# Order of VectorE and ScalarE work at the start of the first delta head in a hybrid decoder trunk

## The reference

```
qkv = silu(causal_conv(qkv_in, conv_w))            # width 4, over time
q = l2norm(q) * B_DK**-0.5;  k = l2norm(k * valid) # 4 heads of 128
beta = sigmoid(beta_in) * valid
log_a = -exp(a_log) * softplus(decay_in + dt_bias)
o = chunk_gated_delta(q, k, v, log_a, beta)        # chunked, WY form
y_b = gated_head_norm(o, g_in, norm_w)             # rmsnorm(o) * silu(gate)
...
ys = stack([y_a, y_b, y_c])
gates = sigmoid(gate_logits)                       # (tokens, 3, D)
merged = sum(gates * (ys @ w_branch), axis=branch)
h = h + merged @ w_out
```

## Time and profile before

| | us |
|---|---|
| median of 3 runs | 1070.21 |
| lowest and highest | 1069.61, 1072.17 |
| the profiled execution, device time | 1069.23 |
| its span, first to last instruction | 1067.4 |
| TensorE busy | 1018.4 (95%) |
| VectorE busy | 552.6 (52%) |
| ScalarE busy | 310.1 (29%) |

### The profile page before, as it was taken

The page is one execution under the profiler, slowest core; times in us unless marked ns, Lnnn a source line. Parts: engine busy times, 40 slices in busy tenths (PEclk is TensorE's granted clock), DMA queues, the critical chain, the costliest instruction groups (busy, mean ns, idle before and its releaser), DMA issues. The chain is left out here.

```text
span 1067.4 us, 20881 instructions
## 1 busy us (share of the span) xinstructions
PE 1018.4 (95%) x8985; PEld 723.0 (68%) x8985; DVE 552.6 (52%) x1088; ACT 310.1 (29%) x579; POOL 112.5 (11%) x109
## 2 busy tenths in 40 slices
PE   9999999989999999999999999999998999787887
PEld 8888888767787877878776676544566665445544
DVE  6577786868569478387464364332344322111114
ACT  2345354624244343344332042010110111100013
POOL 3322222000000000000100100000001222211110
PEclk9999999999999999999999999999999999989899
DMA  9232223231332232142222221174847999999976
GB/s 265 69 85 63 61 61 80 60 64 41 81 64 63 60 84 62 41 88 58 60 60 60 60 61 60 40 275 154 364 163 275 414 415 414 415 416 415 418 312 247
DMA packets 111967, 174.76 MB, mean 164 GB/s; under 512 B 9011, under 2 KB 87100, under 8 KB 103554
## 3 DMA queue, kind: packets, MB, share of 16 engines
q1 hardware_dynamic: 99010, 134.93, 36.6%
q10 hardware_dynamic: 7136, 27.33, 6.5%
q0 software_dynamic: 5728, 11.14, 3.9%
HBM read 169.16 MB, written 12.60 MB: 170 GB/s over the span
## 5 line engine op out<-in xcount | busy, mean ns | idle before, releaser
L823 PE MATMUL ps<-arena 128*128 128x256 f32 x1008 | 237.6, 385 | 0.0
L823 PEld LDWEIGHTS ps<-arena 128*128 128x128 f32 x1008 | 185.2, 190 | 27.3 <-issue 2.8
L1517 DVE TENSOR_TENSOR arena<-arena 128x256 f32<-128x256 f32 (+6 forms) x202 | 111.4, 593 | 49.4 <-ACT arena L1308 32.7
L853 PE MATMUL ps<-arena 128*128 128x264 f32 x400 | 124.3, 393 | 0.8 <-DVE gates L1649 0.8
L2413 PE MATMUL ps<-arena,gates 128*64 128x256 f32 (+1 forms) x1088 | 107.2, 356 | 17.0 <-DMA arena<-in_expert_w_up 16.5
L854 PE MATMUL ps<-arena 128*128 128x264 f32 x400 | 121.7, 386 | 0.0
L2413 PEld LDWEIGHTS ps<-arena,gates 128*64 128x64 f32 x1088 | 74.6, 145 | 55.7 <-DMA arena<-in_expert_w_up 24.9
L847 PE MATMUL ps<-yT,arena 128*128 128x512 f32 x192 | 84.8, 596 | 2.1 <-DVE gates L1649 1.4
L854 PEld LDWEIGHTS ps<-arena 128*128 128x128 f32 x400 | 76.1, 190 | 13.1
L853 PEld LDWEIGHTS ps<-arena 128*128 128x128 f32 x400 | 71.9, 191 | 13.1 <-issue 2.8
L2592 DVE COPY gates<-ps 128x1024 f32<-128x1024 f32 x15 | 18.4, 1224 | 100.9 <-PE ps L2394 100.9
(11 more groups left out here) (379 smaller groups left out, 1396.4 us busy)
## 6 DMA issues: line engine op xcount, KB each, us to landing
arena<-in_w_in SPq DMA_DIRECT2D x68, 512.0 KB, 3.9
arena<-in_expert_w_gate SPq DMA_DIRECT2D x27, 1024.0 KB
arena<-in_expert_w_up SPq DMA_DIRECT2D x27, 1024.0 KB
arena<-in_expert_w_down ACTq DMA_DIRECT2D x16, 1024.0 KB, 34.2
arena<-in_w_branch SPq DMA_DIRECT2D x12, 512.0 KB, 4.2
arena<-in_expert_w_down SPq DMA_DIRECT2D x6, 1024.0 KB, 11.2
C<-in_expert_w_gate SPq DMA_DIRECT2D x5, 1024.0 KB
gates<-in_expert_w_up SPq DMA_DIRECT2D x5, 1024.0 KB
```

The costliest lines, as they stand in the source:

```text
L823: mm = t.matmul(dst, wt[:, k, :], rhs[:, k, :], start=(k == 0), stop=(k == KH - 1))
L853: t.matmul(dst[:, 0:HALF], wt, uT[:, k, 0:HALF], start=(k == 0), stop=(k == KD - 1))
L1517: v.tensor_tensor(out_, a_, b2, op).then_inc(*q.did(name))
```

## The change

The first delta head (r = 0) gets another order; heads 1 to 3 keep theirs. On VectorE, the old head's end (y1, y) and the memset go ahead of the query convolution. That is cut in two: q0 and q1 before the keys' difference tk, q2 and q3 behind it. The gate product and the weight sums S1 and S2 go behind km and kr. On ScalarE the exponential of the merge gate goes from behind the softplus to behind the square kk. `convolve` takes a range of steps for this.

```
--- before.py
+++ after.py
@@ -524,8 +524,9 @@
                                      [f"Z{l}" for l in LB[1:]] + ["nw"])] + each(B_R - 1, ["oo", "ln", "ri"]))
         queries = ["q0", "q1", "q2", "q3"]
         b_dve = Order("b_dve", [x for r in range(B_R) for x in
-                                each(r - 1, ["oq"] if r else []) + each(r, ["k0", "k1", "k2", "k3"]) + (each(r - 1, ["y1", "y"]) if r else each(r, queries + ["pad"])) +
-                                each(r, ["tk", "km", "kr"] + (queries if r else []) + ["dif", "min", "kn", "kb", "Ei", "Es", "tq", "qm", "qr",
+                                each(r - 1, ["oq"] if r else []) + each(r, ["k0", "k1", "k2", "k3"]) + (each(r - 1, ["y1", "y"]) + each(r, ["tk", "km", "kr"] + queries) if r else
+                                                         each(r, ["pad"] + queries[0:2] + ["tk"] + queries[2:] + ["km", "kr"])) +
+                                each(r, ["dif", "min", "kn", "kb", "Ei", "Es", "tq", "qm", "qr",
                                          "U", "Ua", "Ub", "v0", "v1", "v2", "v3", "gc", "kbg", "kd", "tv", "Da", "vm", "vr", "QK", "Db",
                                          "tg", "vb", "qg", "E1", "D1", "g"] +
                                      [x for l in LB[1:] for x in ((f"E{l}", f"D{l}") if l < LEVELS - 1 else (f"E{l}",))] + chain)] +
@@ -1401,12 +1402,12 @@
                 if r == 0:
                     a.wait_ge(*a_dve.after(f"y1.{A_R - 1}"))
                 softplus(b_act, ("abk", "ek", "lk"), r, b_em[:, 0:TOK], b_kbg[:, 0:TOK])
-                if r == 0:
-                    gate_end("a", A_R - 1)
                 a.wait_ge(*b_dve.after(f"tk.{r}"))
                 a.activation(b_em[:, 0:TOK], b_em[:, 0:TOK], ACT.Exp).then_inc(*b_act.did(f"sk.{r}"))
                 a.wait_ge(*b_dve.after(f"kr.{r}"))
                 a.activation(b_kb, b_kf, ACT.Square).then_inc(*b_act.did(f"kk.{r}"))
+                if r == 0:
+                    gate_end("a", A_R - 1)
                 a.wait_ge(*b_pe.after(f"ssk.{r}"))
                 a.activation(b_em, pair(4), ACT.Ln, bias=eps_c).then_inc(*b_act.did(f"lnk.{r}"))
                 a.wait_ge(*b_act.after(f"lnk.{r}"))
@@ -1777,10 +1778,10 @@
                     v.tensor_tensor(q_bg, q_beta, q_eg, ALU.mult).then_inc(*dve0.did("bg"))
                     v.tensor_tensor(q_kd, q_gl, q_g, ALU.subtract).then_inc(*dve0.did("dk"))
 
-            def convolve(s, c, src, r):
+            def convolve(s, c, src, r, steps=range(4)):
                 n = "qkv".index(s)
                 v.wait_ge(*block_done("b", s, r))
-                for j in range(4):
+                for j in steps:
                     at = R_CONV + (3 - j) * 12 + n * 4 + r
                     wc = rowsT[:, at:at + 1]
                     if j == 0:
@@ -1815,16 +1816,23 @@
                 if r:
                     b_finish(r - 1)
                 else:
-                    convolve("q", cq, wide(1), r)
                     a_finish(A_R - 1)
-                    gate_part("a", A_R - 1)
                     v.wait_ge(*a_dve.after(f"y.{A_R - 1}"))
                     v.memset(padding(), 0.0).then_inc(*b_dve.did("pad.0"))
+                    convolve("q", cq, wide(1), r, range(0, 2))
+                if r:
+                    mix_weights("S1", "b", r)
+                less("k", b_em[:, 0:TOK], ck, b_em[:, 0:TOK], r)
+                if r:
+                    mix_weights("S2", "b", r)
+                else:
+                    convolve("q", cq, wide(1), r, range(2, 4))
                     v.wait_ge(*b_dve.after("pad.0"))
-                mix_weights("S1", "b", r)
-                less("k", b_em[:, 0:TOK], ck, b_em[:, 0:TOK], r)
-                mix_weights("S2", "b", r)
                 unit("k", b_kf, ck, b_em, r)
+                if r == 0:
+                    mix_weights("S1", "b", r)
+                    gate_part("a", A_R - 1)
+                    mix_weights("S2", "b", r)
                 if r:
                     convolve("q", cq, wide(1), r)
                 v.wait_ge(sem("decay_rows"), 16 * r + 16)
```

24 lines of the change are left out of this document (15 added, 9 removed).

## The result

| | before | changed |
|---|---|---|
| median, us | 1070.26 (5 runs) | 1064.83 (5 runs) |
| lowest to highest | 1069.61 to 1072.17 | 1062.91 to 1067.21 |
| the profiled execution | 1069.23 | 1067.21 |

The ratio is 0.9946, with an interval of 0.9926 to 0.9967: 5.4 us faster by the medians, where 4.2 were forecast. The same kernel in a second comparison gave 1064.95 against 1069.88, a ratio of 0.9954 (0.9940 to 0.9968). Two executions of the kernel before, in later series, took 1469.5 and 2613.1 us; they are left out of every median here.

The account below looks back on a forecast made before the run. TensorE's own stream was taken as the bound. ssk 3.01 us earlier plus 1.50 from the clock, less a 0.33 wait at the first level product, gave 4.18: median 1070.21 to 1066.0 us, range 1064.2 to 1068.8.

Parts of the forecast that it names:

- What bounds: Whole kernel: TensorE's own stream sets the time; its longest gap, 4.40 us before ssk.0, costs 5.90 with the clock.
- y1 first: VectorE, first delta head: y1 starts when the old head's root is ready, at 229.26 us; softplus then starts 3.49 earlier.
- The steps to ssk: VectorE and ScalarE, y1 through keys to ssk.0: starts 3.01 us earlier, gap 1.39; rival of longer steps, chance 0.12.
- the Trainium skill's rule on the flush: VectorE, split query steps: independent neighbours would save nothing, putting km about 0.1 to 0.2 us later.
- The clock: TensorE between ssk.0 and KK.0: no fall after a 1.39 us gap, giving back 1.50; rival, falls anyway, chance 0.09.
- lnk behind the exponential: ScalarE: lnk waits for the gate's exponential until 238.35 us, costing it 0.7, hidden because kb is ready before KK.
- To the end: Mixers and expert stage: the head's whole 4.18 us gain is kept; rival, no effect or taken back, chance 0.11.

Follow-up runs that it names:

- Fill only: Kernel before with eight instead of six steps of block v ahead of ssk on TensorE in the first delta head; 1067.62 against 1070.01 us, ratio 0.9980.
- the exponential late: Changed kernel with the gate's exponential on ScalarE moved from ahead of lnk to behind the queries' square qq; median 1064.09 us, ratio to before 0.9943.

## Why the prediction was right, point by point

*What bounds.* One serial chain, from the old head's root over y1, softplus, tk, exponential, km, square and ssk to the key norms, sets the head, with TensorE's gap as its sign. "Fill only" shows it: with the clock kept, work in the gap moves the wait to Db.

*y1 first.* y1 started right behind the root. Forecast 229.26, measured 229.40 in a trace that runs 0.13 late. The softplus behind it took 2.08 us; the prediction's 2.09 is not the distance that its rows give (233.59 to 235.58 is 1.99), but nothing hung on it, since VectorE was the later of the two.

*The steps to ssk.* Forecast 3.01 us, measured 3.19. Two steps were shorter than summed and one longer: q0 starts 0.25 behind the memset (the sum had 0.37, read from the weight sum, which waits for the memset, while q0 does not); q0 to q1 took 0.69 (the sum had 0.81); y (230.18) to the memset took 0.83 (the sum had 0.74). The neighbour that does not depend on q1 was worth what the row said: tk 0.68 behind q1 (forecast 0.70). The prediction set against this the Trainium skill's rule on the flush ("VectorE: DVE Perf Modes", section "The DRAIN you can't avoid"), from which it concluded that order saves nothing. That reading was too strong: the same section says that a next operation that is not held starts earlier. The trace agrees with this: q1 to tk 0.68, tk to q2 0.61, against 0.79 from one dependent query step to the next.

*What each part is worth.* The prediction summed the parts in one order and gave none a price of its own. The runs do: 0.4 and 0.6 us alone, 1.0 for the split, and the rest only when the first two are together.

*The clock.* No fall behind the short gap: right in all profiles of the changed kernel, and behind 2.21 us twice. The **mis-sized term** is here: 1.50 us was taken as the price of the fall from the one profile there was, and two others of the same kernel had 2.72 and 2.82, because the clock stayed low for 6.8 us in them and for 3.4 in the first. That is why, as far as three profiles tell, the medians moved by 4.9 and 5.4 us and not by 4.2. The prediction did ask whether the fall would come again; it did not ask whether its price was the same each time, which was a term of the sum and needed a bound. With 1.5 to 2.8 for it the forecast would have been 4.2 to 5.5. Both measured gains lie beyond the forecast's own bounds of 3.6 to 4.8 us; the median, 1064.83, lies in the range only because that had been widened at its lower end for a median of few runs. The mechanism was right; that the size still fell inside was in part luck.

*lnk behind the exponential.* Forecast 238.38, measured 238.22 (238.09 without the offset); the delay against ssk's end was 0.5 us, forecast 0.7 (ssk took 1.35 us, not 1.24, and lnk started 0.1 before the exponential's end). It was called hidden ahead of KK and felt at the first level product, which is what happened: 0.16 of wait, 0.33 forecast. What the sum left out is 0.18 us at the second level product, which took 0.76 and 0.75 us in the two profiles of the changed kernel and 0.56 in the first of the kernel before. With the exponential late, VectorE is 0.5 us sooner there and the product took 0.56, which speaks for VectorE's lateness as the cause. But it took 0.82 in the third profile of the kernel before, and in its second TensorE paused there for 0.25 us of issue, so the cause stays open.

*To the end.* The mixers' loads and the expert stage's moved with TensorE; on the mean of the runs nothing was taken back. That a single execution can lose 2 us there hid half the gain in the profiled one; the prediction had no term for it beyond the 0.7 us that it added for few runs.

## What to carry to other kernels

Where an engine's gap ends a serial chain over three engines, list the chain and ask at each link what it waits for, the operation before it or the queue in front of it; here two links were late for two reasons, and mending one alone moved ssk by 0.4 or 0.6 us of 3.2. An operation that two others wait for goes ahead of bulk work (y1 before the queries), bulk work that nobody waits for goes into the waits of the chain (two query steps over the exponential, the gate product behind the keys), and cutting a block of four in two made it fit. Before a term is taken from a profile, look whether it can differ between executions: a fall of the clock is such a term. And if a gap costs the clock, moving work into it that is due anyway is the cheaper first try.

## What the runs showed of the hardware

Gaps on TensorE and the granted clock behind them: 1.21 us (three profiles) and 2.21 us (two) kept 1.00; 2.62 us kept it once and lost it once, with the same kernel; 3.83, 4.00 and 4.40 us lost it each time (five profiles). The same gap of 4.40 cost 1.50, 2.72 and 2.82 us of TensorE's time, with the clock at 0.50 for 3.4 us in the first and 6.8 in the others. In the case of 2.62 that lost it, the clock fell 1.4 us after TensorE had taken up its work again, so the first product behind a gap can still run at 2.4 GHz. The gap of 2.54 us in the expert stage did the same: work starts at 950.93, and the clock is at 1.00 to 952 us and 0.61 on the mean of the next microsecond. The Trainium skill says that the monitor's window is free-running ("TensorE: Matmul & The Clock Gate", section "What's actually happening"); by that rule one and the same gap can cost differently in different executions, and the traces agree: 7.80, 9.12 and 9.02 us for the same work. It stood beside the prediction as an argument on whether the clock falls; it bears as much on what a fall costs.
